# Second layer's heads: work moved from VectorE to ScalarE, value products as three fp32r products

## The reference, cut to what matters

```python
dmat = jnp.where(order, b[..., :, None] - b[..., None, :] + ig[..., None, :], -jnp.inf)
inter = b + m[..., None]
m_t = jnp.maximum(inter, jnp.max(dmat, axis=-1))
s = jnp.einsum('bhtd,bhsd->bhts', q, k) * jnp.exp(dmat - m_t[..., None])
...
num = a[..., None] * jnp.einsum('bhtd,bhde->bhte', q, C) + jnp.einsum('bhts,bhse->bhte', s, v)
den = a * jnp.einsum('bhtd,bhd->bht', q, n) + jnp.sum(s, axis=-1)
h = num / jnp.maximum(jnp.abs(den), jnp.exp(-m_t))[..., None]
...
y = jax.nn.sigmoid(o.astype(f32)).reshape(B, T, M_HEADS, M_DV) * h
y = _rmsnorm(y, hn.reshape(M_HEADS, M_DV)).reshape(B, T, M_V).astype(z.dtype)
return (y * jax.nn.silu(z)) @ w_out
```

## Time and profile before

| | us |
|---|---|
| median of 3 runs | 2987.8 |
| lowest and highest of them | 2987.46 and 2990.23 |
| profiled execution, its own time | 2990.57 |
| span of the profiled execution | 2988.8 |
| TensorE busy in the span | 2932.5 (98%) |
| VectorE busy | 2090.1 (70%) |
| ScalarE busy | 1178.0 (39%) |
| GpSimd busy | 103.5 (3%) |

### The profile page before, as it was taken

How to read it: one execution, slowest core, us unless ns; L and a number is a source line. 1 busy time by engine, 2 the same in 40 slices (tenths; PEclk the granted TensorE clock), 3 DMA queues, 4 the chain that set the end, 5 groups by cost and what they waited for, 6 DMA issues and landing times.

```text
span 2988.8 us, 43582 instructions
## 1 busy us (share of the span) xinstructions
PE 2932.5 (98%) x17098; PEld 2353.5 (79%) x17098; DVE 2090.1 (70%) x3957; ACT 1178.0 (39%) x2056; POOL 103.5 (3%) x188
## 2 busy tenths in 40 slices
PE   8999999999999999999999999999999999999999
PEld 7777778888888888878888888888888888885346
DVE  4576876788888776677666886677675678765455
ACT  4322323322332232242245555455444445543344
POOL 0000000000000000000000000000010120000000
PEclk9999999999999999999999999999999999999999
DMA  9777784354555455538636774645576443487997
GB/s 366 281 266 286 273 282 149 127 169 148 190 168 177 162 183 169 179 128 275 235 117 206 258 241 142 197 148 180 195 236 218 141 164 128 152 274 259 403 404 314
DMA packets 193197, 641.69 MB, mean 215 GB/s; under 512 B 21488, under 2 KB 36192, under 8 KB 192992
## 3 DMA queue, kind: packets, MB, share of 16 engines
q1 hardware_dynamic: 132080, 423.44, 40.6%
q10 hardware_dynamic: 58032, 207.12, 20.3%
q0 software_dynamic: 2880, 8.35, 0.9%
HBM read 624.15 MB, written 12.58 MB: 213 GB/s over the span
## 4 chain that ended last, share of the span: by engine, by line
PE 87%; DVE 7%; ACT 3%; DMA 2%; issue 1%; SPq 0%; DVEq 0%; ACTq 0%; POOL 0%; POOLq 0%
PE PS L506 15%; PE PS L502 11%; PE PS L504 9%; PE PS L505 9%; PE PS L635 7%; PE PS L637 7%; PE PS L636 7%; PE PS L1061 2%; PE PS L798 2%; PE PS L1472 2%; DMA AR<-e_w 1%; DVE WL L2389 1%; PE PS L1441 1%; PE PS L1428 1%; PE PS L1122 1%
## 5 line engine op out<-in xcount | busy, mean ns | idle before, releaser
L2389 DVE TENSOR_TENSOR WL<-WR,WH 128x1024 fp32r<-128x1024 f32 (+1 forms) x566 | 682.4, 1211 | 401.7 <-ACT WH L1574 400.5
L506 PE MATMUL PS<-HT,WL 128*128 128x256 f32 (+1 forms) x2928 | 951.5, 325 | 0.0
L1574 ACT ACTIVATE WH<-WR 128x1024 fp32r<-128x1024 f32 (+1 forms) x566 | 587.1, 1044 | 873.1 <-PE PS L506 486.7
L506 PEld LDWEIGHTS PS<-HT,WL 128*128 128x128 f32 x2928 | 552.1, 189 | 47.6
L502 PE MATMUL PS<-HT,WH 128*128 128x512 f32 x1584 | 566.0, 401 | 9.2 <-DVE WL L2389 6.1
L504 PE MATMUL PS<-HT,WH 128*128 128x512 f32 (+1 forms) x1344 | 518.4, 386 | 5.4 <-DVE HT L2369 2.4
L505 PE MATMUL PS<-HT,WH 128*128 128x512 f32 (+1 forms) x1344 | 507.9, 378 | 0.0
L635 PE MATMUL PS<-WH,HT 128*128 128x512 f32 x1016 | 402.7, 396 | 3.5 <-DVE HT L2369 2.5
L637 PE MATMUL PS<-WH,HT 128*128 128x512 f32 x1016 | 396.8, 391 | 0.0
L636 PE MATMUL PS<-WL,HT 128*128 128x512 f32 x1016 | 396.2, 390 | 0.0
L502 PEld LDWEIGHTS PS<-HT,WH 128*128 128x128 f32 x1584 | 297.4, 188 | 90.2 <-issue 13.1
(11 more groups left out here) (472 smaller groups left out, 3319.1 us busy)
## 6 DMA issues: line engine op xcount, KB each, us to landing
WR<-ada_w SPq DMA_DIRECT2D x264, 512.0 KB, 4.6
AR<-e_w SPq DMA_DIRECT2D x88, 512.0 KB, 10.0
E_RING<-e_w SPq DMA_DIRECT2D x80, 512.0 KB, 10.2
WR<-m_vo ACTq DMA_DIRECT2D x64, 512.0 KB, 4.6
WR<-a_qz ACTq DMA_DIRECT2D x64, 512.0 KB, 4.8
WR<-n_m SPq DMA_DIRECT2D x64, 512.0 KB, 4.3
AR<-ada_p ACTq DMA_DIRECT2D x56, 512.0 KB, 6.3
AR<-ada_p SPq DMA_DIRECT2D x48, 512.0 KB, 8.0
```

The lines of the kernel that those rows point to most:

```text
L506: return e.matmul(ps[:, 0:b - a], wl, HH_[:, c, a:b], start=False, stop=c == last)
L1574: e.activation(part_of(WH, s), place_of(plan["slot"][p])[:, 0:width(s)], ACT.Copy, scale=1.0).then_inc(*L.up(hi_done, ("hi", s)))
L2389: e.tensor_tensor(part_of(WL, s), place_of(plan["slot"][plan["split"][s]])[:, 0:width(s)], part_of(WH, s).bitcast(F32), ALU.subtract).then ...
```

## The change

For the eight heads of the second layer:

- M_P, M_V are written also as a high part rounded to fp32r (M_PH, M_VH) and a low part (M_PL, M_VL, the difference); each fp32 value product of 257 columns becomes three fp32r products of 258 columns (two columns of ones, zeros in the low part).
- ACT adds the column term out of PSUM: the diagonal blocks as a plain sum (`Identity` with a bias; POOL then fills the triangle with -3e38, and ACT takes the exponential afterwards), the other blocks at once through `Exp` with a bias. The clamp at 0 is gone. Only the blocks that `M_KEYS` uses are multiplied by `S` and split (`M_BLOCKS`).
- ACT writes the high parts of M_P, scales the forward direction's bank into M_HH, and does the last scaling of M_HH; before the tanh of each bank of `vo` it writes the high part of the values. VectorE writes the low parts.
- The two half-blocks behind `k(h+1)` move into `along_vo`, one more behind each of the pieces 2 and 5 (not for head 0's `vo`).

```diff
+    M_VH, M_VL = (ARR[:, at:at + 1032].rearrange("p (t n) -> p t n", t=4) for at in (2048, 11784))
+    M_PH = [ARR[:, 8712 + 1536 * d:10248 + 1536 * d] for d in range(2)]
+    M_PL = [ARR[:, 5128 + 1536 * d:6664 + 1536 * d] for d in range(2)]
...
+    M_BLOCKS = {(0, 0): [(0, 512)], (0, 1): [(0, 128), (256, 512)], (1, 0): [(128, 512)], (1, 1): [(0, 512)],
+                (2, 0): [(256, 512)], (2, 1): [(256, 384)], (3, 0): [(384, 512)], (3, 1): [(256, 512)]}
+    M_REST = {(0, 0): [(128, 512)], (0, 1): [(256, 512)], (1, 0): [(256, 512)], (1, 1): [(0, 128), (256, 512)],
+              (2, 0): [(384, 512)], (2, 1): [], (3, 0): [], (3, 1): [(256, 384)]}
...  tensor_program
-                            i = e.matmul(ps[:, 0:257], M_P[d][:, c:c + 128], M_V[:, k, :], start=m == 0,
-                                         stop=m == len(ks) - 1)
+                            e.matmul(ps[:, 0:258], ph, M_VH[:, k, :], start=m == 0, stop=False)
+                            e.matmul(ps[:, 0:258], ph, M_VL[:, k, :], start=False, stop=False)
+                            i = e.matmul(ps[:, 0:258], pl, M_VH[:, k, :], start=False, stop=m == len(ks) - 1)
...  scalar_program: vo(h), then the head
+                    e.activation(M_VH[:, tb, 0:256], place[("vo", h, tb)][:, 0:256], ACT.Copy, scale=1.0)
                     e.activation(M_O[:, tb, :], place[("vo", h, tb)][:, 256:512], ACT.Tanh, scale=0.5)
...
+                for d in range(2):
+                    for k in range(4):
+                        e.activation(M_P[d][:, m_at(k, t.start, t.stop)], ps[:, t], ACT.Identity,
+                                     bias=M_ACOL[:, k, 32 * d + h:32 * d + h + 1], scale=1.0)
+                    for k in range(4):
+                        for a, b in M_REST[k, d]:
+                            e.activation(M_P[d][:, m_at(k, a, b)], ps[:, a:b], ACT.Exp,
+                                         bias=M_ACOL[:, k, 32 * d + h:32 * d + h + 1], scale=1.0)
                 for k in range(4):
-                    n = 512 if k < 2 else 256
                     for d in range(2):
-                        p = M_P[d][:, M_PC[k]:M_PC[k] + n]
-                        w.wait_ge(L.at(("pt", h, k, d)))
+                        p = M_P[d][:, m_at(k, 128 * k, 128 * k + 128)]
+                        w.wait_ge(L.at(("pa", h, k, d)))
                         e.activation(p, p, ACT.Exp, scale=1.0)
                 for k in range(4):
+                    for d in range(2):
+                        w.wait_ge(L.at(("pp", h, k, d)))
+                        for a, b in M_BLOCKS[k, d]:
+                            e.activation(M_PH[d][:, at], M_P[d][:, at], ACT.Copy, scale=1.0)
                     if k == 0 and h:
                         z_(2 * h)
...
+                for tb in range(4):
+                    w.wait_ge(L.at(("pvs", h, tb, 0)))
+                    e.activation(M_HH[:, tb, :], place[("pv", h, tb, 0)][:, 0:256], ACT.Copy,
+                                 scale=M_ST[2 * tb % 4][:, 0:1])
...  behind the root
+                w.wait_ge(L.at(("yi", h)))
+                for tb in range(4):
+                    e.activation(M_HH[:, tb, :], M_HH[:, tb, :], ACT.Copy, scale=s[:, 8 + tb:9 + tb])
...  vector_program
-                    copy(M_V[:, tb, 0:256], place[("vo", h, tb)][:, 0:256], ("ve", h), ("free", ("vo", h, tb)))
+                    tt(M_VL[:, tb, 0:256], place[("vo", h, tb)][:, 0:256], M_VH[:, tb, 0:256].bitcast(F32), ALU.subtract,
+                       ("ve", h), ("free", ("vo", h, tb)))
...
-                    bg(1)
+                    bg(2 if q in (2, 5) and h else 1)
...
+                def lows(k):
+                    for d in range(2):
+                        w.wait_ge(L.at(("ph", h, k, d)))
+                        for a, b in M_BLOCKS[k, d]:
+                            at = m_at(k, a, b)
+                            tt(M_PL[d][:, at], M_P[d][:, at], M_PH[d][:, at].bitcast(F32), ALU.subtract, ("p", h, k, d))
                 for k in range(4):
+                    if k:
+                        lows(k - 1)
                     for d in range(2):
-                        ts(p, place[("cb", h, d)][:, c0:512], M_ACOL[:, k, 32 * d + h:32 * d + h + 1], 0.0,
-                           ALU.add, ALU.min, ("pt", h, k, d), *([("free", ("cb", h, d))] if k == 3 else []))
-                for k in range(4):
-                    for d in range(2):
-                        w.wait_ge(L.at(("pa", h, k, d), ("full", ("S", h, k))))
-                        tt(p, p, place[("S", h, k)][:, 0:512 - c0], ALU.mult, ("p", h, k, d), ("free", ("S", h, k)))
+                        w.wait_ge(L.at(("pe", h, k, d), ("full", ("S", h, k))))
+                        for a, b in M_BLOCKS[k, d]:
+                            tt(p, p, place[("S", h, k)][:, a - c0:b - c0], ALU.mult, ("pp", h, k, d), ("free", ("S", h, k)))
...
                     elif k == 3 and h < 7:
                         along(("k", h + 1))
-                        bg(2)
+                lows(3)
                 for tb in range(4):
                     for d in range(2):
...
-                        if d == 0:
-                            scaled(M_HH[:, tb, :], ps[:, 0:256], s, ALU.mult, ("free", ("pv", h, tb, d)))
-                        else:
+                        if d:
+                            w.wait_ge(L.last(dve_done), L.at(("pvx", h, tb)))
                             stt(M_HH[:, tb, :], ps[:, 0:256], s, M_HH[:, tb, :], ALU.mult, ALU.add,
...
-                recip(s[:, 8:12], s[:, 8:12])
-                w.wait_ge(L.last(dve_done))
-                for tb in range(4):
-                    scaled(M_HH[:, tb, :], M_HH[:, tb, :], s[:, 8 + tb:9 + tb], ALU.mult, ("yn", h, tb))
+                recip(s[:, 8:12], s[:, 8:12], ("yi", h))
```

More of the change, by code:

```diff
@@ L1886, in vo @@
                     w.wait_ge(L.at(("o_used", h - 1)))
+                    w.wait_ge(L.at(("v_used", h - 1)))
                 for tb in range(4):
+                    e.activation(M_VH[:, tb, 0:256], place[("vo", h, tb)][:, 0:256], ACT.Copy, scale=1.0).then_inc(
+                        *L.up(act_done, ("vh", h, tb)))
                     e.activation(M_O[:, tb, :], place[("vo", h, tb)][:, 256:512], ACT.Tanh, scale=0.5).then_inc(
@@ L1922, in mlstm @@
                         k_(h + 1)
+                if h:
+                    w.wait_ge(L.at(("hh_used", h - 1)))
+                for tb in range(4):
+                    w.wait_ge(L.at(("pvs", h, tb, 0)))
+                    e.activation(M_HH[:, tb, :], place[("pv", h, tb, 0)][:, 0:256], ACT.Copy,
+                                 scale=M_ST[2 * tb % 4][:, 0:1]).then_inc(
+                        *L.up(act_done, ("pvx", h, tb), ("free", ("pv", h, tb, 0))))
                 s = M_ST[h % 4]
@@ L2897, in vo @@
                     w.wait_ge(L.at(("v_used", h - 1)))
+                else:
+                    one = ONE[:, 0:8].rearrange("p (t n) -> p t n", t=4)
+                    copy(M_VH[:, :, 256:258], one)
+                    tt(M_VL[:, :, 256:258], one, one, ALU.subtract)
                 for tb in range(4):
-                    w.wait_ge(L.at(("oe", h, tb)))
-                    copy(M_V[:, tb, 0:256], place[("vo", h, tb)][:, 0:256], ("ve", h), ("free", ("vo", h, tb)))
+                    w.wait_ge(L.at(("vh", h, tb), ("oe", h, tb)))
+                    tt(M_VL[:, tb, 0:256], place[("vo", h, tb)][:, 0:256], M_VH[:, tb, 0:256].bitcast(F32), ALU.subtract,
+                       ("ve", h), ("free", ("vo", h, tb)))
             def along_vo(h, first):
@@ L3835, in mlstm @@
             for h in range(8):
-                for k in range(4):
-                    g0 = 128 * k - (0 if k < 2 else 256)
-                    for d in range(2):
-                        pd = M_P[d][:, M_PC[k] + g0:M_PC[k] + g0 + 128]
+                for d in range(2):
+                    for k in range(4):
+                        pd = M_P[d][:, m_at(k, 128 * k, 128 * k + 128)]
                         sg = 1 if d == 0 else -1
-                        w.wait_ge(L.at(("pe", h, k, d)))
-                        e.affine_select(out=pd, in_=pd, compare_op=ALU.is_ge, fill=0.0, base=0,
+                        w.wait_ge(L.at(("pt", h, k, d)))
+                        e.affine_select(out=pd, in_=pd, compare_op=ALU.is_ge, fill=-3e38, base=0,
                                         pattern=[[sg, 128]], channel_multiplier=-sg).then_inc(
```

43 lines of the change are left out of this document (26 added, 17 removed).

## The result

| | kernel before | changed kernel |
|---|---|---|
| median of 14 runs each, us | 2987.71 | 2991.03 |
| lowest and highest | 2980.84 and 2990.23 | 2987.34 and 3002.23 |
| ratio of the changed kernel to the one before | | 1.0014 (95% interval 1.0007 to 1.0020) |
| second set (17 and 12 runs): medians | 2987.34 | 2991.81 |
| ratio in the second set | | 1.0016 (1.0008 to 1.0025) |

The change makes the kernel slower by 3 to 5 us, inside the 0.2% that I had called the bound of one measurement, but above no change in both sets. I had forecast 3.5 us less: 2984.3 is 6.7 us too low, and the sign is wrong.

A forecast was written before the change was run, and what follows sets the result against it. TensorE, busy 99.4 to 100 of every 100 us in the heads, was taken as the bound. Terms -14.7 + 6.8 + 4.4 = -3.5 us took the median 2987.8 to 2984.3; its own range was 2980 to 2990.

The forecast's parts named there:

- The value products: Each head's value products: 60 fp32r products at 0.12 us, wait gone; 5 x 2.34 + 2 x 1.49 = 14.7 us gained.
- What vo pays: Vo stage: ten half-blocks held up by loads make TensorE wait at starts of heads 1 to 4; 6.8 us lost.
- E: Reference point in each head: the end of vo, where the transposes start; times are counted from it.
- 4 x 1.7 = 6.8 us lost: Starts of heads 1 to 4: TensorE waits 1.7 us each for VectorE's reading of the transposes' first bank.
- What the head's start pays: From E: the new VectorE - ScalarE - VectorE loop fits with 0.4 to 1 us to spare; costed at nothing.
- The loop is longer than the turn: Rival, chance 0.17: way from VectorE's products over ScalarE to the weight's low part too long in early heads; +7.2, 2995.
- Head 7: Head 7, no projections behind k = 1 to 3: the new chain lies open; 4.4 us lost, bounds 2 to 7.
- The sum: All terms together: -14.7 + 6.8 + 4.4 = -3.5 us, 2984.3 against the median.
- Elsewhere: Theory held after the first profile, not in the prediction: the gain is lost in a later stage.
- The loads keep up: Rival, chance 0.30: places in vo reloaded within 4.3 us, no waits at heads' starts; -10.3, 2977.5.

The follow-up runs named there:

- the mends: Changed kernel with four half-blocks put off to heads 5 and 6, tanh ahead of the high-part copy, head 7 reordered: 2972.73 us, ratio 0.9953.
- e9_fp32_products: Kernel with the mends, its three fp32r value products made one fp32 product of the high parts: 2983.62 us, ratio 0.9986 to the kernel before.
- e3_head7: Changed kernel with head 7's four scores in a row, then z(14), its weights and gate behind the low parts, two half-blocks moved out: 2991.82 us.
- e5_tanh: Changed kernel with one half-block per early head behind k = 3's low parts, plus tanh ahead of each bank's high-part copy: 2980.39 us.
- e6_later: Changed kernel with nine half-blocks in vo for heads 1 to 4, four more behind k = 3's low parts in heads 5 and 6: 2984.67 us.
- e10_wait: Kernel before, with three unused copies of the transposes' first bank ahead of VectorE's reading in heads 0 to 3: 2996.27 us, ratio 1.0029.
- e11_all_again: Second run of the changed kernel with the mends, for its profile: 2973.92 us, ratio 0.9961 to the kernel before.
- e2_warm: Changed kernel with the row-term product of d = 1 done eight times more in heads 1 to 4, filling TensorE's waits: 2989.05 us, ratio 1.0006.

## Why the prediction was wrong

**The value products: right.** Forecast -2.34 us in each of heads 0 to 4; head 0, which has no wait at its start, went from 88.44 to 86.10, and with the mends heads 1 to 4 from 101.07 to 98.73. Late heads: forecast -1.49, measured -1.10 in the changed kernel, whose tanh wait of 0.34 us stands in the period, and -1.53 for head 6 with the tanh mended. e9_fp32_products gives the same size from the other side (+10 for a forecast of 10.4). TensorE went by the row of 120 ns; the Trainium skill's 110 ns (TensorE: Matmul & The Clock Gate, Back-to-back issue gap), a formula that by the page's own words leaves out weight loads, of which each product here has one, and the 4 us more that I estimated from it were not seen.

**What vo pays: the failing step, in its size.** The mechanism happened as written: ten half-blocks held up by their loads, the tenth ending 2.85 us after E (forecast 2.6), TensorE waiting at the starts of heads 1 to 4. But the term "4 x 1.7 = 6.8 us lost" was too small twice. The waits were 7.5 us in the first profile and 9.8 in the second, 1.9 and 2.5 each on average. And it took the price of a wait to be its length: behind it TensorE ran at the lower clock, once of four in the first profile, four of four in the second and in e3_head7, 1.4 to 1.6 us each time. Together 9.1 us in the first (7.5 + 1.6) and 15.8 in the second (9.8 + 6.0). The prediction's text says the granted clock is 1.00 in the heads and never asks what a wait does to it.

**What the head's start pays: costed at nothing, and wrong by ScalarE's table load.** I had the load in the list, "between the first copy and the first tanh (1.28)", and compared only the late end of that chain with TensorE's due times. The near end is z(2h): its first bank is one that tanh frees. TensorE waited 0.34 us for it in three heads, and in seven once the other waits were gone. e5_tanh shows the load's price where it isn't covered: 4 to 5.5 us. The rival "The loop is longer than the turn" did not come: no wait for a weight's low part stands in the turns, and with the mends the period is what the products alone make it.

**Head 7: right.** Forecast +4.4, measured 41.01 - 36.37 = +4.64. VectorE finished the low parts at 1308.25, E + 23.9 as forecast, and z(15) started at 1314.43 (forecast E + 30.0 = 1314.34). The lower clock behind the wait of 4.4 us, which I had not reckoned with, added next to nothing here: the products that it slowed would have waited for the first bank anyhow, and that came free at 1309.21, E + 24.87 (forecast 24.95).

**The sum.** Forecast for the heads -3.5. First profile: -0.1, of whose 3.4 us over the forecast 0.7 are longer waits at the starts, 1.6 the clock, 0.8 heads 5 and 6 with their tanh, 0.2 head 7. Second: +6.7, of whose 10.2 us over the forecast 3.0 are longer waits at the starts, 6.0 the clock, 0.4 a fifth, short wait at head 5's start, 0.4 head 6 with its tanh, 0.2 head 7; 0.2 I can't place. The medians (+3.3 and +4.5) lie between the two. The bounds that I gave (starts at 1.0 to 2.8, head 7 at 2 to 7) add up to -8.7 to +3.5, not to the -8 to +2 that I wrote. 'Elsewhere' falls: outside the heads both executions took the same (2987.34 - 729.54 = 2257.8 us and 2994.25 - 736.34 = 2257.9), so what separates them lies inside. The kernel before took 2260.9 us there in its profiled execution, and the profiles of all kernels here run from 2254.9 to 2261.1, though they hardly differ there: two single executions can be some microseconds apart for reasons outside the heads, and these are not followed up here. The rival that was to end slower was not the one that did; "The loads keep up" was the wrong way round.

**What stays open.** Which waits the lower clock follows. In seven profiles (the two of the changed kernel, e3_head7, e6_later, e9_fp32_products, e10_wait, e11_all_again) 19 waits of 1.49 to 2.96 us stand at a head's start, and it followed 11 of them: not one of 2.38 us, but one of 1.76. It followed all eight in two executions of these heads and one of four in two others. Nor is it settled why the loads land later in some executions. How much of the median is the one and how much the other is known only roughly (e2_warm: some 2 us for the falls).

## What to carry to other kernels

Where TensorE sets the time, price a new wait of it not by its length alone, but also for the case that it runs the next microseconds at the lower clock, and look at more than one profiled execution before believing either. Work that is moved out of one place for a reason (here the half-blocks behind k) needs a place with room to land: counting pieces against the turnaround of their loads told where it would not fit. Putting them off to heads whose pieces were half as long cleared four heads and still held up a fifth; moving one of them inside each head was worth as much by itself (1.8 and 2.1 us below the kernel before of its set). A table load belongs in front of a wait and not behind it: put the operation that needs the table first.

## What the runs showed of the hardware that was not expected

The granted clock dropped to its lower level behind waits of TensorE as short as 1.76 us in one execution and held at 1.00 behind waits of 2.24 and 2.38 us in others. Behind a wait at a head's start the fall lasted for 2 to 8 projection matmuls, at 0.43 us instead of 0.23, and at times took in the score products ahead of them. In all 11 cases it cost 1.4 to 1.6 us, and the cost did not grow with the wait's length (1.76 to 2.96 us).

A half-block's load of 512 KB into a place just freed took about 5 us in the earlier trace rows; with ten instead of eight half-blocks in vo the total that VectorE waited for such loads in heads 0 to 4 was 14.8 us in one execution and 17.6 in another of the same kernel; with the eight of the kernel before it was 1.0.
